# Norm stages merged into the projections behind them, gate tiles in halves, 512-column products and constant products in TensorE's waits

## The chip, the cores and the metric

The kernel runs on one core of one Trainium2 chip. The metric is the device time of one execution in microseconds (us). Three runs of the kernel before gave 1825.0, 1827.96 and 1829.33 us, median 1827.96 us.

## The reference

Two transformer blocks act on x (256 tokens, width 1024), all in float32. What matters here are the places where a norm stands ahead of a projection:

```python
h = x
h = h + hybrid_mixer(rmsnorm(h, norm_mix[l]), w_in[l], ...)      # norm 1 -> projection in_t
h = h + peer_ffn(rmsnorm(h, norm_ffn[l]), peer_wq[l], ...)       # norm 2 -> projection wq
x = rmsnorm(h, norm_final)                                       # final norm
h = jnp.concatenate([meta, x], axis=1)                           # 16 + 256 tokens
u = rms_norm(h, attn_norm_w) @ attn_w_in                         # norm 3 -> projection attn_t
# banded attention with sinks over 16 heads, output (o * silu(gate)) @ w_out, gate = last 1024 columns of u
h = h + attention
u = rms_norm(h, dn_norm_w) @ dn_w_in                             # norm 4 -> projection dn_in
# gated delta rule in chunks of 64 tokens, last product @ dn_w_out
return h[:, 16:]
```

`rmsnorm(x, g)` is `x * rsqrt(mean(x*x) + 1e-6) * g`, by row.

## The kernel before

Every weight matrix is cut into tiles of 128 x 1024 (512 KB) that one ring of four buffers takes in the order of use. ScalarE makes the high part of a tile (`make_high`, L166, a copy to fp32r recorded at L175), VectorE or, for half of the tiles of `dn_in`, GpSimd the low part (`make_low`, L178, L187). Both parts have two buffers. A float32 product is the sum of three fp32r products: high x high, high x low, low x high. `tile_T` (L215) issues them for one weight tile as 16 matmuls on the high part (L222) and 8 on the low part (L226), each with 256 or 272 columns of activations, high or low part. `k.pair(cols)` names the activations' two parts.

The program is a sequence of blocks. A block holds one instruction list for each engine, in the order that the code writes, and no engine goes on to the next block before all are done with this one.

`norm_stage` (L249) is a block of its own, used four times: ScalarE squares each row tile (L271, 128 x 1024 with a running sum), VectorE takes the mean (L288), ScalarE the root (L275, with a load of its table), VectorE refines the inverse root and writes it times the identity (L294 to L300), TensorE multiplies each 128-column chunk of the rows with this diagonal, which turns and scales them (L314, plain fp32; row tile by row tile, chunks inside), and ScalarE and VectorE write the high (L281) and low (L306) parts of the 8 chunks. `early(k, following)` makes the parts of the next projection's first two tiles in the same block, except for the first norm. `project_T` (L320) is the block behind: one `tile_T` for each output chunk, and a copy from PSUM.

`final_norm_stage` (L1368) is another block between `experts_out_stage` (L1255) and norm 3: it loads three arrays, squares the rows (L1386), takes root and Newton step (L1389, `newton` at L1403) and multiplies the rows by root and weight (L1399).

`sink_attention_stage` (L1470) works through 16 units (2 row tiles tt of 128 tokens, 8 pairs of heads each). In iteration u TensorE issues `scores(u + 2)` (L1509), for u < 8 one whole tile of the gate's projection through `tile_T` into bank 7, then `values(u - 1)` (L1536) and `turn(u)` (L1521). ScalarE takes the exponentials (L1605, L1608), makes tile parts, copies the gate tile from PSUM (L1637), stores values and turned scores, and at u = 10 applies Silu to the whole gate (L1644). Units with tt = 1 have more keys, so their matmuls have more columns.

`out_rows` (L2776) is the output projection (L2845, 512 columns), with a residual add by VectorE in two halves of 512 columns (L2829). It runs ahead of norm 2 and of norm 4, and last with the output. `delta_stage` (L1999) ends with the last chunk: `last_within` (L2189), a norm, `last_turn_out` (L2197).

## Time and profile before

| | |
|---|---|
| median of three runs | 1827.96 us |
| the profiled execution | 1824.91 us, span of its trace 1823.0 us |
| granted TensorE clock, mean | 0.949 of full |
| TensorE matmul, weight load | 1672.1 us (92%), 1493.9 us (82%) |
| VectorE, ScalarE, GpSimd | 1183.5 us (65%), 895.0 us (49%), 70.0 us (4%) |
| DMA | 230 MB, mean 126 GB/s |

All times inside the program are counted from the start of the span. The projected and expert tiles follow one another on TensorE almost without a gap; the gaps lie around the norms, in the attention of the second block and at the end of the delta rule. Busy shares are means over the whole program and say little of one stage, so the stages are read by windows and by the order of instructions in time.

### The profile page before, as it was taken

What the parts mean: (1) busy time and instruction counts of PE and PEld (TensorE: products, weight loads), DVE (VectorE), ACT (ScalarE), POOL (GpSimd) and SP (SyncE); (2) the same over time, 40 slices, a digit from 0 to 9 for tenths busy, and PEclk for the clock granted to TensorE, in tenths of its full rate; (3) what the DMA queues carried; (4) which work ended last, traced back from release to release, by engine and by line L of the source; (5) the groups of instructions that cost most, each with busy time, mean ns of one, the idle gap of its engine ahead of it and who ended that gap; (6) DMA issues with size and microseconds to landing.
All of it is one profiled execution on the core that took longest, in us unless ns stands there. A gap on an engine that the chain in (4) does not pass through costs nothing. (4 is left out here: it accounts for less than half of the span.)

```text
span 1823.0 us, 34509 instructions
## 1 busy us (share of the span) xinstructions
PE 1672.1 (92%) x13270; PEld 1493.9 (82%) x13270; DVE 1183.5 (65%) x2021; ACT 895.0 (49%) x1554; POOL 70.0 (4%) x35
## 2 busy tenths in 40 slices
PE   5989988899999999989999999687987999898979
PEld 5978777899999999988888888584656988788877
DVE  3556654478989699976666666544633757546665
ACT  3335543244555677756666666432643644333323
POOL 0000000010000000000000000000000333200000
PEclk9979988999999999999999999796978999999989
DMA  5532143455555444436666656431112444300004
GB/s 181 177 117 82 58 129 124 141 166 169 176 170 173 150 128 128 128 116 194 189 194 194 195 189 193 132 128 35 59 47 69 139 150 151 104 3 3 3 25 138
DMA packets 63078, 230.03 MB, mean 126 GB/s; under 512 B 7009, under 2 KB 7265, under 8 KB 62833
## 3 DMA queue, kind: packets, MB, share of 16 engines
q1 hardware_dynamic: 62960, 228.39, 39.5%
q8 instruction: 83, 1.36, 0.3%
q14 instruction: 35, 0.28, 0.0%
HBM read 227.32 MB, written 1.05 MB: 125 GB/s over the span
## 5 line engine op out<-in xcount | busy, mean ns | idle before, releaser
L974 DVE TENSOR_TENSOR tile_low<-weights,tile_high 128x1024 fp32r<-128x1024 f32 x252 | 307.2, 1222 | 146.4 <-ACT tile_high L964 142.2
L964 ACT ACTIVATE tile_high<-weights 128x1024 fp32r<-128x1024 f32 x252 | 269.1, 1068 | 136.7 <-issue 136.7
L175 ACT ACTIVATE tile_high<-weights 128x1024 fp32r<-128x1024 f32 x169 | 178.1, 1059 | 271.8 <-PE banks L222 106.3
L187 DVE TENSOR_TENSOR tile_low<-weights,tile_high 128x1024 fp32r<-128x1024 f32 x146 | 179.7, 1237 | 187.3 <-ACT tile_high L175 154.2
L222 PE MATMUL banks<-parts,tile_high 128*128 128x272 f32 (+1 forms) x1904 | 266.9, 294 | 14.5 <-PEq L262 6.8
L1026 PE MATMUL banks<-parts,tile_high 128*128 128x256 f32 x2048 | 272.7, 286 | 6.9 <-PEq L900 6.9
L222 PEld LDWEIGHTS banks<-parts,tile_high 128*128 128x128 f32 x1904 | 248.0, 194 | 32.0 <-issue 25.1
L1026 PEld LDWEIGHTS banks<-parts,tile_high 128*128 128x128 f32 x2048 | 257.1, 194 | 7.1 <-issue 7.1
L1308 PE MATMUL banks<-tile_high,parts 128*128 128x512 f32 x1024 | 254.7, 391 | 4.7 <-ACT parts L1288 4.7
L1308 PEld LDWEIGHTS banks<-tile_high,parts 128*128 128x128 f32 x1024 | 193.3, 189 | 45.1 <-issue 4.9
L1031 PE MATMUL banks<-parts,tile_low 128*128 128x256 f32 x1024 | 146.7, 286 | 9.2 <-DVE tile_low L974 9.2
L1031 PEld LDWEIGHTS banks<-parts,tile_low 128*128 128x128 f32 x1024 | 133.0, 193 | 12.3 <-DVE tile_low L974 11.8
L226 PE MATMUL banks<-parts,tile_low 128*128 128x272 f32 (+1 forms) x952 | 137.9, 288 | 0.9 <-DVE tile_low L187 0.9
L1308 PE MATMUL banks<-tile_low,parts 128*128 128x512 f32 x512 | 137.5, 391 | 0.0
L226 PEld LDWEIGHTS banks<-parts,tile_low 128*128 128x128 f32 x952 | 126.8, 192 | 1.1 <-DVE tile_low L187 1.1
L1308 PEld LDWEIGHTS banks<-tile_low,parts 128*128 128x128 f32 x512 | 96.7, 189 | 20.2
L1080 ACT ACTIVATE big<-banks 128x256 f32 (+1 forms) x79 | 52.8, 668 | 120.1 <-PE banks L1031 120.1
L1101 ACT ACTIVATE rows<-rows,kept 128x128 f32<-128x128 f32 x256 | 80.2, 393 | 24.8 <-DVE rows L1182 24.6
L1288 ACT ACTIVATE parts<-big 128x256 fp32r (+1 forms) x128 | 87.6, 686 | 4.3 <-PEq L1007 4.3
L2845 PE MATMUL banks<-tile_high,parts 128*128 128x512 f32 (+1 forms) x288 | 77.4, 417 | 7.2 <-ACT parts L2805 4.1
L1325 DVE TENSOR_TENSOR parts<-big,parts 128x256 fp32r<-128x256 f32 x128 | 81.3, 636 | 1.0 <-ACT parts L1288 1.0
L1182 DVE TENSOR_TENSOR rows<-const,kept 128x1024 f32<-128x1024 f32 x64 | 76.5, 1219 | 0.0
(357 smaller groups left out, 1984.3 us busy)
## 6 DMA issues: line engine op xcount, KB each, us to landing
weights<-in_peer_u SPq DMA_DIRECT2D x128, 512.0 KB, 3.5
weights<-in_peer_v SPq DMA_DIRECT2D x128, 512.0 KB, 3.5
weights<-in_dn_in SPq DMA_DIRECT2D x49, 512.0 KB, 3.5
weights<-in_in_t SPq DMA_DIRECT2D x19, 512.0 KB, 3.6
weights<-in_attn_t SPq DMA_DIRECT2D x19, 512.0 KB, 3.6
weights<-in_in_m SPq DMA_DIRECT2D x16, 512.0 KB, 3.6
weights<-in_wq SPq DMA_DIRECT2D x16, 512.0 KB, 3.5
weights<-in_dn_out SPq DMA_DIRECT2D x16, 512.0 KB, 3.5
```

The lines of the kernel that those rows point to most:

```text
L175: k.nc.scalar.activation(k.high[:, m % 2, :], k.ring.view(n), ACT.Copy).then_inc(*k.high_made.up())
L187: unit.tensor_tensor(k.low[:, m % 2, :], k.ring.view(n), k.high[:, m % 2, :].bitcast(F32), ALU.subtract).then_inc(*k.low_made[engine].up())
L222: ins = nc.tensor.matmul(out, high[:, c, :], rhs(c)[part], start=part + c == 0, stop=False)
L226: ins = nc.tensor.matmul(out, low[:, c, :], rhs(c)[0], start=False, stop=c == chunks - 1)
L964: k.nc.scalar.activation(k.high[:, (s + j) % 2, :], k.ring.buf[:, j % RING, :], ACT.Copy).then_inc(k.high_made.sem, 1)
L974: k.nc.vector.tensor_tensor(k.low[:, (s + j) % 2, :], k.ring.buf[:, j % RING, :], k.high[:, (s + j) % 2, :].bitcast(F32), ALU.subtract).th ...
L1026: ins = nc.tensor.matmul(ps[:, bank, 0:S], high[:, c, :], x[:, c, :], start=part + c == 0, stop=False)
L1031: ins = nc.tensor.matmul(ps[:, bank, 0:S], low[:, c, :], k.pair(S)[0][:, c, :], start=False, stop=c == KC - 1)
L1101: nc.scalar.activation(hot, hot, ACT.Copy, scale=k.chosenT[:, 2, Q * g + q:Q * g + q + 1]).then_inc(*scaled.up())
L1288: nc.scalar.activation(stage[:, j % STAGES, :], c_of(i, j), ACT.Copy).then_inc(staged.sem, 1)
L1308: ins = nc.tensor.matmul(ps[:, 2 * tt + half, :], c[:, j % STAGES, tt * P:tt * P + P], v[:, half, :], start=head and j + part == 0, stop=t ...
L1325: nc.vector.tensor_tensor(stage_low[:, j % STAGES, :], c_of(i, j), stage[:, j % STAGES, :].bitcast(F32), ALU.subtract).then_inc(staged_low ...
```

## The change

- `norm_stage` becomes `norm_programs`, which returns instruction lists; `project_T` and `delta_in_stage` run them at the head of their own block. There is no block boundary between norm and projection, and the first projection tile waits for the parts chunk by chunk.
- The diagonal products run chunk by chunk, row tiles inside (a 16-row tile ahead of them, where there is one). Root and Newton step are taken once for all row tiles, by `newton`.
- `out_rows` squares the halves of the rows right behind the residual adds, makes the first tile of the next projection and loads the table of the root with a one-column Sqrt. `experts_out_stage` does the same, and the whole of what is left of the final norm: it multiplies by the final weight only, squares before and behind it, and the two inverse roots are worked out together in norm 3. The rows are stored without the final norm's factor; the residual add behind the attention multiplies it in.
- `tile_both` replaces `tile_T` where the projection has 256 columns (`in_t`, 19 tiles, `wq`, 16 tiles): both parts of the activations are one moving operand of 512 columns. A sum of the two halves (`tensor_reduce`) replaces the copy from PSUM.
- The gate's tiles in the attention are issued in halves of 12 matmuls (`tile_piece`), one in each of the 16 iterations; Silu runs in iteration 16.
- `keep_busy` issues fp32 matmuls of 384 columns of constants: 3 at the head of norms 2 to 4, 4 behind each of the two `out_rows` ahead of a norm, 8 behind the experts, 5 and 2 in the last chunk.

```diff
+def tile_both(pe, k, n, out, cols, norm=None):
+    x, _ = k.pair(cols)
+    both = k.parts[:, :, 0:KC * cols].rearrange("p a (c n) -> p a c n", c=KC)
+    await_high(pe, k, n)
+    for c in range(KC):
+        if norm is not None:
+            pe.wait_ge(*norm["left"].at(c + 1))
+        ins = nc.tensor.matmul(out[:, 0:2 * cols], high[:, c, :], both[:, :, c, :], start=c == 0, stop=False,
+                               skip_group_check=True)
+    ins.then_inc(*k.high_used.up())
+    await_low(pe, k, n)
+    for c in range(KC):
+        ins = nc.tensor.matmul(out[:, 0:cols], low[:, c, :], x[:, c, :], start=False, stop=c == KC - 1,
+                               skip_group_check=True)
+    tile_used(ins, k, n)
+def sum_halves(k, out, both):
+    return k.nc.vector.tensor_reduce(out, both.rearrange("p (a n) -> p n a", a=2), AX.X, ALU.add)
+def keep_busy(k, bank, times):
+    for _ in range(times):
+        k.nc.tensor.matmul(k.ps[:, bank, 0:3 * P], k.ident, k.common[:, 0:3 * P], start=True, stop=True)
...
+    def scalar(act):
+        if not halves:
...
+        act.wait_ge(*chain.at(3 if scaled_rows else 2 if halves else 1))
+        nc.scalar.activation(root, y, ACT.Sqrt).then_inc(*rooted.up())
+        for m in ahead:
+            make_high(act, k, m)
+        for c in range(KC):
+            act.wait_ge(*turned.at(c + 1))
+            nc.scalar.activation(high[:, c, :], ps[:, c, 0:cols], ACT.Copy,
+                                 scale=weight[:, c:c + 1]).then_inc(*parted.up())
...
+    def tensor(pe):
+        if halves:
+            keep_busy(k, 7, 3)
+        if t > NT:
+            pe.wait_ge(*scaled.at(1))
             for c in range(KC):
+                product(0, c)
+        pe.wait_ge(*scaled.at(t))
+        for c in range(KC):
+            for i in range(t - NT, t):
+                ins = product(i, c)
+            ins.then_inc(*turned.up())
...
@@ experts_out_stage, ScalarE and VectorE behind the last round
+            act.wait_ge(*got.at(32))
+            nc.scalar.activation(scratch[0:META, 0, :], k.hm[0:META, :], ACT.Square,
+                                 accum_out=sums[0:META, 0:1]).then_inc(*squared.up())
+            nc.scalar.activation(k.norms[:, 47:48], k.ident[:, 0:1], ACT.Sqrt).then_inc(*squared.up())
+            make_high(act, k, k.tiles["attn_t"])
+            for tt in range(NT):
+                act.wait_ge(*added.at(tt + 1))
+                nc.scalar.activation(scratch[:, tt, :], k.h[:, tt, :], ACT.Square,
+                                     accum_out=sums[:, 1 + NT + tt:2 + NT + tt]).then_inc(*squared.up())
+            for tt in range(NT):
+                act.wait_ge(*weighted.at(tt + 1))
+                nc.scalar.activation(scratch[:, tt, :], k.h[:, tt, :], ACT.Square,
+                                     accum_out=sums[:, 1 + tt:2 + tt]).then_inc(*squared.up())
...
+            for tt in range(NT):
+                dve.wait_ge(*squared.at(3 + tt))
+                nc.vector.tensor_tensor(k.h[:, tt, :], k.h[:, tt, :], wide, ALU.mult).then_inc(*weighted.up())
+            make_low(dve, k, k.tiles["attn_t"])
...
@@ sink_attention_stage
-                if u < fills:
-                    if u:
-                        pe.wait_ge(*gated.at(u))
-                    tile_T(pe, k, gate_tile(u), fill, lambda c: (high[:, c, :], low[:, c, :]))
+                if u < 2 * fills:
+                    if u and u % 2 == 0:
+                        pe.wait_ge(*gated.at(u // 2))
+                    tile_piece(pe, k, gate_tile(u // 2), fill, lambda c: (high[:, c, :], low[:, c, :]), u % 2, 2)
...
-                if u == fills + 2:
+                if u == len(units):
                     act.wait_ge(*gated.at(fills))
                     nc.scalar.activation(T[:, GATE:GATE + fills, :], T[:, GATE:GATE + fills, :],
                                          ACT.Silu).then_inc(*gated.up())
...
@@ delta_stage, TensorE, last chunk
             for b in range(2):
                 last_within(b)
+            keep_busy(k, 0, 5)
             for b in range(2):
                 last_turn_out(b)
+            keep_busy(k, 0, 2)
...
@@ out_rows (send is None ahead of norms 2 and 4)
+            if send is None:
+                make_high(act, k, k.tiles[following])
+                nc.scalar.activation(k.norms[:, 47:48], k.ident[:, 0:1], ACT.Sqrt).then_inc(*squared.up())
+                for half in range(2):
+                    for i, (h, _, rows, _) in enumerate(tiles):
+                        act.wait_ge(*added.at(len(tiles) * half + i + 1))
+                        nc.scalar.activation(scratch[0:rows, half, i, :], h[0:rows, 512 * half:512 * half + 512], ACT.Square,
+                                             accum_out=k.norms[0:rows, 40 * half + i:40 * half + i + 1]).then_inc(*squared.up())
...
+                if half == 0 and send is None:
+                    make_low(dve, k, k.tiles[following])
...
+            if send is None:
+                keep_busy(k, 7, 4)
```

On TensorE, from the end of the first block's output projection to the first tiles of `wq`, the order was, before (L2845 output projection, L314 diagonal products of norm 2, L222 and L226 the tiles of `wq`):

```order
L2845 MATMUL banks<-tile_high,parts 128x512 x8
L2845 MATMUL banks<-tile_low,parts 128x512 x4
L2785 UNCONDITIONAL_BRANCH
L309 UNCONDITIONAL_BRANCH
L314 MATMUL banks<-rows 128x128 x16
L262 UNCONDITIONAL_BRANCH
L335 UNCONDITIONAL_BRANCH
L222 MATMUL banks<-parts,tile_high 128x256 x16
L226 MATMUL banks<-parts,tile_low 128x256 x8
```

and is now (L2932 output projection, L281 `keep_busy`, L368 diagonal products, L245 and L250 `tile_both`):

```order
L2932 MATMUL banks<-tile_high,parts 128x512 x8
L2932 MATMUL banks<-tile_low,parts 128x512 x4
L281 MATMUL banks<-const 128x384 x4
L2857 UNCONDITIONAL_BRANCH
L402 UNCONDITIONAL_BRANCH
L281 MATMUL banks<-const 128x384 x3
L368 MATMUL banks<-rows 128x128 x16
L245 MATMUL banks<-parts,tile_high 128x512 x8
L250 MATMUL banks<-parts,tile_low 128x256 x8
```

One block boundary (two branches) is gone, seven constant matmuls have come, and a tile has 16 matmuls instead of 24.

On ScalarE at the same place, before (L175 tile parts, L2805 activations' parts, L271 squares, L275 root, L281 parts of the normed rows):

```order
L2805 ACTIVATE parts<-big 128x512
L175 ACTIVATE tile_high<-weights 128x1024 x2
L2785 UNCONDITIONAL_BRANCH
L268 UNCONDITIONAL_BRANCH
L271 ACTIVATE rows,small<-rows 128x1024 x2
L275 ACT_TABLE_LOAD
L275 ACTIVATE small<-small 128x1 x2
L175 ACTIVATE tile_high<-weights 128x1024 x2
L281 ACTIVATE parts<-banks,param 128x256 x8
```

and now (L2882 one-column Sqrt, L2887 squares of halves, L331 root, L336 parts):

```order
L2877 ACTIVATE parts<-big 128x512
L175 ACTIVATE tile_high<-weights 128x1024 x3
L2882 ACT_TABLE_LOAD
L2882 ACTIVATE norms<-const 128x1
L2887 ACTIVATE rows,norms<-rows 128x512 x4
L2857 UNCONDITIONAL_BRANCH
L424 UNCONDITIONAL_BRANCH
L331 ACTIVATE norms<-norms 128x2
L175 ACTIVATE tile_high<-weights 128x1024
L336 ACTIVATE parts<-banks,param 128x256 x8
```

Table load, squares and one tile's parts stand ahead of the boundary now; behind it are one root, one tile's parts and the eight chunks.

On TensorE in the attention, iterations 9 and 10 (tt = 1) were, before (L1536 values, L1521 turned scores, L1509 scores):

```order
L1509 MATMUL banks<-big 128x272 x2
L1536 MATMUL banks<-big 64x128 x6
L1521 MATMUL banks<-const,big 16x128 x2
L1521 MATMUL banks<-const,big 128x128 x4
L1509 MATMUL banks<-big 128x272 x2
L1536 MATMUL banks<-big 64x128 x6
```

and are now (L1574 scores, L270 the gate's tile in halves, L1599 values, L1586 turned scores):

```order
L1574 MATMUL banks<-big 128x272 x2
L270 MATMUL banks<-parts,tile_high 128x272 x4
L270 MATMUL banks<-parts,tile_low 128x272 x8
L1599 MATMUL banks<-big 64x128 x6
L1586 MATMUL banks<-const,big 16x128 x2
L1586 MATMUL banks<-const,big 128x128 x4
L1574 MATMUL banks<-big 128x272 x2
L270 MATMUL banks<-parts,tile_high 128x272 x12
L1599 MATMUL banks<-big 64x128 x6
```

Twelve matmuls of a gate tile stand between scores and values in the second half of the units, where none stood; in the first half twelve stand where 24 stood.

## Rows read from the trace of the kernel before

**Rows 1.** Waits of TensorE: who for whom, us in total, times, longest.
```profile
PE banks L314 <- DVE rows L300: 44.9, 4, 15.7
...
PE banks L2197 <- DVE rows L2440: 4.4, 1, 4.4
```
**Rows 2.** Windows: length, busy (count) of PE, PEld, DVE, ACT, POOL, clock, DMA, GB/s.
```profile
812.00:1164.00 352.00, 350.75 (x1536) 289.95 (x1536) 225.83 (x255) 209.65 (x254) 0.00 (x0) 0.99 0.61 191
1310.00:1350.00 40.00, 31.62 (x172) 19.18 (x172) 19.68 (x72) 22.54 (x64) 0.00 (x0) 0.83 0.00 1
```
**Rows 3.** Timeline around norm 2: start, length, engine, instructions, [idle before and releaser].
```profile
286.98 1.28 DVE L2829 TENSOR_TENSOR rows<-rows,banks 128x512 f32<-128x512 f32 x2 [1.43 <-PE banks L2845]
...
290.77 1.28 ACT L275 ACT_TABLE_LOAD   x1
...
293.42 6.45 PE L314 MATMUL banks<-rows 128*128 128x128 f32 x32 [6.47 <-DVE rows L300]
...
301.82 3.33 PE L222 MATMUL banks<-parts,tile_high 128*128 128x256 f32 x16 [1.96 <-PEq L262]
...
306.26 2.08 PE L222 MATMUL banks<-parts,tile_high 128*128 128x256 f32 x16
...
309.14 2.08 PE L222 MATMUL banks<-parts,tile_high 128*128 128x256 f32 x16
```
**Rows 4.** Timeline, fp32 matmuls of 272 columns ahead of the attention, two records each.
```profile
1241.52 9.33 PE L1453 MATMUL banks<-big,const 20*64 20x272 f32 x40 [4.58 <-DVE big L1413]
```
**Rows 5.** Timeline around norm 1.
```profile
14.76 5.87 PE L314 MATMUL banks<-rows 128*128 128x128 f32 x32 [14.76 <-DVE rows L300]
...
15.25 0.35 DVE L300 TENSOR_SCALAR rows<-const,small 128x128 f32<-128x128 f32 x1
...
27.12 2.08 PE L222 MATMUL banks<-parts,tile_high 128*128 128x256 f32 x16
```
**Rows 6.** Timeline from the experts over final norm and norm 3.
```profile
1163.57 2.35 DVE L1334 TENSOR_TENSOR rows<-rows,banks 128x1024 f32<-128x1024 f32 x2 [3.88 <-PE banks L1308]
...
1166.22 1.06 ACT L1386 ACTIVATE rows<-rows 128x1024 f32<-128x1024 f32 x1 [7.88 <-PEq L1270]
...
1169.72 0.20 ACT L1389 ACTIVATE small<-small 128x2 f32<-128x2 f32 x1
...
1170.75 0.16 DVE L1413 TENSOR_TENSOR small<-small 128x2 f32<-128x2 f32 x1
...
1194.06 2.16 PE L222 MATMUL banks<-parts,tile_high 128*128 128x272 f32 x16
```
**Rows 7.** Timeline of TensorE in the attention: a gate tile, then units without one.
```profile
1275.53 2.27 PE L222 MATMUL banks<-parts,tile_high 128*128 128x272 f32 x16
...
1278.73 1.51 PE L1536 MATMUL banks<-big 16*64 16x128 f32 x8
...
1313.98 1.95 PE L1536 MATMUL banks<-big 16*64 16x128 f32 x12 [0.43 <-ACT big L1619]
...
1317.78 1.95 PE L1536 MATMUL banks<-big 16*64 16x128 f32 x12 [0.43 <-ACT big L1619]
...
1324.69 3.39 PE L1536 MATMUL banks<-big 16*64 16x128 f32 x12 [3.55 <-ACT big L1619]
...
1330.60 3.39 PE L1536 MATMUL banks<-big 16*64 16x128 f32 x12
```
**Rows 8.** The same timeline of ScalarE: Silu of the gate.
```profile
1319.04 2.02 ACT L1644 ACTIVATE big<-big 128x2176 f32<-128x2176 f32 x1
```
**Rows 9.** Timeline around norm 4.
```profile
1387.99 1.87 DVE L2829 TENSOR_TENSOR rows<-rows,banks 16x512 f32<-16x512 f32 x3 [2.30 <-PE banks L2845]
...
1412.58 2.16 PE L222 MATMUL banks<-parts,tile_high 128*128 128x272 f32 x16
```
**Rows 10.** Timeline of TensorE in the last projection.
```profile
1772.85 3.75 PE L2845 MATMUL banks<-tile_high,parts 128*128 128x512 f32 x8 [1.87 <-ACT parts L2805]
...
1777.57 2.01 PE L2845 MATMUL banks<-tile_high,parts 128*128 128x512 f32 x8
```

More of the change, by code:

```diff
@@ L258, in norm_stage @@
     starts = [sum(rows for _, rows in tiles[:i]) for i in range(len(tiles))]
[L259 to L260 removed]
+    t = len(tiles)
+    n = t + NT if scaled_rows else t
+    sums, y, root, inv, step = (k.norms[:, 8 * a:8 * a + n] for a in range(5))
+    scratch = k.mid[:, (3 - t) * D:3 * D].rearrange("p (t n) -> p t n", n=D)
     diagonal = lambda i: scratch[0:tiles[i][1], i, 0:tiles[i][1]]
[L262 to L269 removed]
+    ahead = range(k.tiles[following] + (1 if halves else 0), k.tiles[following] + AHEAD)
```

269 lines of the change are left out of this document (137 added, 132 removed).

## The prediction

> **What bounds the kernel now.** The busy shares come first: TensorE is busy 92% of the span, every other engine far less, so time is won where TensorE stands idle, runs at the lower clock, or issues more than it must. The list of its waits comes next. Its largest entry by far is norm: the diagonal products waited 44.9 us in all for VectorE's diagonals, four times [rows 1]. The windows then tell good stretches from bad ones. In the second half of the experts TensorE is busy 350.75 of 352 us at clock 0.99 [rows 2]: 1536 matmuls of 512 columns, 0.229 us each, and 191 GB/s of weights come in behind them. In the second half of the attention it is busy 31.62 of 40 us, at 0.83 [rows 2]. The timeline around one norm shows what a wait is made of: the output projection ends where VectorE begins its last adds, 286.98, and the second tile of `wq` starts at 306.26 [rows 3]. Between lie adds, squares, a table load of 1.28 us, root and Newton step, products at 0.40 us each (6.45 us for 16), the last parts, a block boundary, and a first tile that takes 4.4 us where its successor takes 2.88 (306.26 to 309.14) [rows 3]. The products and that first tile ran at the lower of the clock's two levels, 1.2 GHz, after TensorE had idled.
>
> **Unit prices.** A projection tile of 24 matmuls with 256 columns takes 2.88 us [rows 3], 0.120 each; one with 512 columns costs 0.229 [rows 2]. An fp32 matmul is two records; 40 records of 272 columns take 9.33 us [rows 4], 0.86 ns a column and record, so a product of 128 columns costs 0.22 us at the upper clock, and one of `keep_busy` with 384 columns 0.66. A block boundary costs 0.3 us (VectorE ends at 1165.92, ScalarE starts at 1166.22) [rows 6]. From the root's start to the end of the Newton step are 1.2 us (1169.72 to 1170.91) [rows 6]; a small VectorE step in a chain 0.2; a diagonal 0.35 [rows 5], a second one chained behind it 0.6 for both.
>
> **Norm 2.** The last add ends at 288.26 [rows 3]. ScalarE squares the last half behind it, 0.7 us (half of L1386's 1.06 and the read of the sum [rows 6]), to 289.0. The four constant matmuls run from 286.95 to 289.6 and so set the end of the block; they cost 0.6 us. With the boundary it is 289.9. Two small steps, root and Newton, two diagonals: 0.45 + 1.2 + 0.6, products from 292.15. They are 16 x 0.22 = 3.5 us at the upper clock, since three constant matmuls fill 289.9 to 291.9. Parts are made beside them, chunk by chunk, and the first tile's parts are there. Its first matmul comes at 295.7, its end 8 x 0.229 + 8 x 0.120 = 2.8 us later at 298.5, against 306.26. **7.7 us.** If the upper clock does not hold, the products take their old 6.45 us and the tile up to 1.5 more: 3.3 us are left.
>
> **Norm 1.** Nothing changes ahead of it, and it has no constant matmuls. Products wait for both diagonals, 0.5 us later than 14.76, and take 5.87 as before [rows 5], to 21.1. The wait for the last parts, a boundary, and the late making of the first tile's parts go: tile 0 ends at 23.9, against 27.0 [rows 5]. **3.1 us.** Its weights are among the first four tiles, which the input block already loads.
>
> **512 columns.** A tile goes from 2.88 to 2.79 us by these prices. The mean over 1536 matmuls holds the stage's start and loop turns, so I take 0.227 and 2.77: 0.11 x 33 further tiles = 3.6, less 0.5 for two sums at projection ends that are longer than copies. **3.1 us.** VectorE has a low part of 1.2 us and a sum of about 0.7 in each tile and stays hidden. Weights must come at 189 GB/s, below the 191 of the experts [rows 2].
> The Trainium skill, page "TensorE: Matmul & The Clock Gate", section "Back-to-back issue gap", gives N/2.4 + 2.5 ns for a matmul. By it 8 matmuls of 512 columns in place of 16 of 256 would save only 8 x 2.5 ns = 0.02 us a tile, under 1 us in all. Rows 2 and 3 disagree: both widths carry 13 to 16 ns over their columns at 2.4 GHz. By the rule the sum would be 3 us smaller.
>
> **Final norm and norm 3.** TensorE stops at 1163.5; adds end at 1165.92 [rows 6]. The square of the first row tile (1.1) runs beside the second add, that of the second ends at 1167.1. VectorE weights both tiles (1.2 each, as its adds) to 1168.4, ScalarE squares the second by 1169.6; VectorE's low part ends there too. Eight constant matmuls end at 1168.8 and are covered. Boundary: 1169.9. Three small steps, root, Newton, three diagonals 0.65 + 1.2 + 0.9: 1172.7. The eight products of the 16-row tile start at 1172.2 and take 1.8 us, the 16 others 3.5: 1177.5. The first tile, 24 x 0.125 = 3.0, ends at 1180.5, against 1194.06 [rows 6]. **13.5 us.** It goes to 10.5 if the products run at the lower clock. The loads move: final weight and meta rows are fetched 350 us earlier, ahead of the experts' fifth tile, when four tiles lie ready; the block of constants goes ahead of `attn_t`'s fifth tile.
>
> **Attention.** A unit with tt = 1 has 3.37 us of matmuls (period 3.80 from 1313.98 to 1317.78, less the wait of 0.43) [rows 7]. Silu (2.02 us [rows 8] and two table loads) holds the exponentials back: TensorE waits 3.55 us, and comes back at the lower clock, two units at 5.91 us (1324.69 to 1330.60) instead of 3.37 [rows 7]. Window 1310 to 1350 thus holds 8.4 us idle and 2 x 2.54 = 5.1 of slow clock [rows 2, 7]. Half gate tiles fill the waits: what stood in the first half, where TensorE was full, now stands here. Of 13.5 us I take off 2: cutting tiles in two costs something (a gate tile takes 3.20, 1275.53 to 1278.73 [rows 7], 0.2 more than the 3.0 of 24 x 0.125 elsewhere, paid at most once more for each of eight tiles), and nothing stands behind the last unit to fill its wait. Silu now runs behind the last copy, 1.28 + 2.02 + the last store 0.3, where values took 2.3: the block ends 1.3 us later. **10 us.** VectorE has peaks and scale, 2.5 to 3.0 us a unit, and every second unit 1.2 more; a unit lasts 4.1 to 5.0, so TensorE stays the bound. If the chain over make_high and make_low does bind in the first half, 1 us in each of 8 units comes back: down to 2.
>
> **Norm 4.** As norm 2 with three row tiles: last add 1389.86 [rows 9], square and boundary to 1391.0, chain 0.45 + 1.2 + 0.9, eight small products (1.8, half of them beside the diagonals) and 16 others (3.5) to 1398.3, first tile to 1401.3, against 1412.46 [rows 9]. **11.2 us**; 7 at the lower clock.
>
> **Last chunk.** Five constant matmuls, 3.3 us, stand in the wait of 4.4 us for the norm [rows 1], and two, 1.3 us, ahead of the wait of 1.87 for the next parts [rows 10]. The first tile of the last projection takes 4.7 us (1772.85 to 1777.57) [rows 10], a warm one 2.72. **2 us**, or nothing.
>
> **Sum:** 7.7 + 3.1 + 3.1 + 13.5 + 10 + 11.2 + 2 = 50.6 us. The profiled execution took 1824.9 us, 3 below the median of 1828.0; taken off the median it gives 1777.4, off this execution 1774.3. I forecast **1777 us**.
>
> **Rivals.**
> *A: the clock falls all the same.* TensorE then works through norms 2 to 4 and the last tile at 1.2 GHz: 4.4 + 3 + 4.2 + 2 = 13.6 us less gained, 1791. (4.4 is 7.7 less 3.3.) For it: in norm 2 the clock fell again behind products that had just ended, within 2 us of idleness [rows 3]. Against it: the constants leave gaps of 0.3 and 1.3 us only, and fp32 products brought the clock back in norm 1. Chance 0.17. The skill's page, section "Part 1: The HAM clock gate", says that activity releases the throttle and that its phase is not tied to the kernel; the traces agree with the first, and the second would put A between runs rather than in all.
> *B: attention's chain binds.* ScalarE's high part waits behind exponentials, VectorE's low part behind it, peaks behind that; TensorE waits about 1 us a unit: 8 us less, 1785. Against it: the same chain stood in every iteration before, with a whole tile to make in each, and the list of waits has no entry of that size for it. Chance 0.13.
> *C: 512 columns save nothing* by a per-matmul cost of 3 ns instead of 13: 1780. Chance 0.10.
> *D: slower.* The moving operand is two pieces of 256 columns that lie apart; no row here shows such an operand. Were it streamed at half rate, each of 280 matmuls would cost 0.227 us more, 64 us in all: 1841. It decides from 0.18 us more a matmul. The sum over two strided halves would add to that. Chance 0.02.
> *E: the table of the root is lost* between the one-column Sqrt and the root, so 3 loads of 1.28 return: 1781. Against it: the order lists no load there. Chance 0.03.
> The forecast as it stands has 0.55.
>
> **Numbers.** The forecast's own bounds are 1770 (boundaries and waits also gone elsewhere, cheaper attention) to 1784. The range of 1766 to 1791 takes in B, C, E and A's middle. A measurement tells about 0.2%, 3.7 us, from no change; all cases but D lie far below: faster 0.97, same 0.01, slower 0.02.
>
> **What would show it.** Right: TensorE's first tile starts 5.5 to 6 us behind the boundary of norms 2 and 4, 7.5 behind that of norm 3, with granted clock near 1; tile periods of 2.77 us in `in_t` and `wq`; attention from first gate matmul to last values about 75 us instead of 86; no wait for exponentials over 1 us. Wrong: diagonal products at 0.43 us each (A), waits of the turned scores on VectorE in every unit (B), periods of 2.88 (C) or above 4 us (D), a table load ahead of the root (E).

## The result, and the profile after

The changed kernel took 1779.01 us (median of four runs, 1776.18 to 1780.42) against 1826.74 us for the kernel before, measured in turn with it (1825.0 to 1829.33): a ratio of 0.9736, 95% interval 0.9718 to 0.9754. The forecast was 1777 us: 50.6 us taken off the first median of the kernel before, 1827.96; the two medians here differ by 47.7. The profiled execution took 1776.18 us, with a span of 1774.4 us (before: 1823.0) and a mean granted clock of 0.971 (before: 0.949).

The list of TensorE's waits, as in [rows 1]. The four waits for diagonals, 44.9 us, have become two, of which one is the start of the program:

```profile
PE banks L368 <- DVE rows L356: 17.2, 2, 15.3
...
PE banks L2200 <- DVE big L2402: 7.1, 5, 2.0
```

The other of the two is the 1.89 us at norm 4. Around norm 2, to set beside [rows 3], the timeline of TensorE and VectorE reads:

```profile
281.57 2.74 PE L281 MATMUL banks<-const 128*128 128x384 f32 x8
281.77 1.28 DVE L2914 TENSOR_TENSOR rows<-rows,banks 128x512 f32<-128x512 f32 x2 [0.30 <-PE banks L2932]
...
284.61 2.17 PE L281 MATMUL banks<-const 128*128 128x384 f32 x6 [0.30 <-PEq L2857]
...
286.84 3.84 PE L368 MATMUL banks<-rows 128*128 128x128 f32 x32
...
290.44 2.09 PE L245 MATMUL banks<-parts,tile_high 128*128 128x512 f32 x8
...
293.32 2.00 PE L245 MATMUL banks<-parts,tile_high 128*128 128x512 f32 x8
...
296.11 2.00 PE L245 MATMUL banks<-parts,tile_high 128*128 128x512 f32 x8
```

The products take 3.84 us for 32 records (6.45 before), the first tile starts 5.83 us behind the boundary at 284.61, and tiles follow at 2.79 us (293.32 to 296.11). Norm 3, to set beside [rows 6], has the same picture: constants, 48 records of products in 5.72 us, and the second tile at 1165.15. In norms 2 to 4 no table load stands between the one-column Sqrt and the root.

```profile
1147.73 5.32 PE L281 MATMUL banks<-const 128*128 128x384 f32 x16
...
1154.31 2.17 PE L281 MATMUL banks<-const 128*128 128x384 f32 x6 [1.26 <-PEq L1347]
...
1156.53 5.72 PE L368 MATMUL banks<-rows 16*128 16x16 f32 x48
```

Norm 4 does not. Here VectorE, GpSimd and TensorE in order of time, to set beside [rows 9]:

```profile
1351.38 3.58 POOL L1898 MEMSET big<- 128x768 f32 x4 [769.83 <-POOLq L2857]
...
1351.62 0.54 DVE L352 TENSOR_SCALAR norms<-norms 128x3 f32<-128x3 f32 x1
...
1352.49 0.18 DVE L1470 RECIPROCAL norms<-norms 128x3 f32<-128x3 f32 x1 [0.34 <-ACT norms L331]
1352.70 0.16 DVE L1472 TENSOR_TENSOR norms<-norms 128x3 f32<-128x3 f32 x1
...
1353.10 1.88 DVE L1476 TENSOR_SCALAR norms<-norms 128x3 f32<-128x3 f32 x1
...
1355.49 7.35 PE L368 MATMUL banks<-rows 16*128 16x16 f32 x48 [1.89 <-DVE rows L356]
...
1365.73 2.17 PE L227 MATMUL banks<-parts,tile_high 128*128 128x272 f32 x16
```

A step of three numbers a partition takes 1.88 us where its neighbours take 0.16 to 0.18. It ends at 1354.98, where the fourth fill by GpSimd ends (1351.38 + 3.58 = 1354.96). The step of 0.54 us ends at 1352.16 with the first fill, which takes 0.76 us. TensorE runs out of constants, idles 1.89 us, and its products take 7.35 us instead of norm 3's 5.72: the granted clock is 1.00 up to 1357 and 0.50 from 1359 to 1361. In the kernel before, the same fills ran behind the norm, beside the first tile of `dn_in` (1407.97):

```profile
1407.93 0.62 POOL L1830 MEMSET rows<- 48x640 f32 x1 [812.19 <-POOLq L262]
1408.51 3.55 POOL L1833 MEMSET big<- 128x768 f32 x4
```

In the attention, to set beside [rows 2, 7], the window of the second half, and three of TensorE's rows near its end:

```profile
1270.00:1310.00 40.00, 37.94 (x261) 27.48 (x259) 23.39 (x73) 25.99 (x69) 0.00 (x0) 1.00 0.11 36
```
```profile
1303.29 1.95 PE L1599 MATMUL banks<-big 16*64 16x128 f32 x12
...
1307.08 1.95 PE L1599 MATMUL banks<-big 16*64 16x128 f32 x12 [1.09 <-ACT big L1682]
1312.39 4.86 PE L2932 MATMUL banks<-tile_high,parts 128*16 128x512 f32 x11 [3.36 <-ACT parts L2877]
```

TensorE is busy 37.94 of 40 us at clock 1.00 (before: 31.62 at 0.83), and the one wait for an exponential or turned score that is left, ahead of the last values, takes 1.09 us.

Read off at the same events in both traces, the stretches changed by these amounts (us):

| stretch | before | after | gained | predicted |
|---|---|---|---|---|
| start to second tile of `in_t` (norm 1) | 27.12 | 24.24 | 2.9 | 3.1 |
| the further tiles of `in_t` and `wq` (512 columns) | 53.95 + 44.14 | 52.66 + 43.11 | 2.3 | 3.1 |
| last output matmul to second tile of `wq` (norm 2) | 19.70 | 11.99 | 7.7 | 7.7 |
| last experts' matmul to second tile of `attn_t` (final norm, norm 3) | 30.92 | 17.66 | 13.3 | 13.5 |
| first scores to output projection (attention) | 90.49 | 79.83 | 10.7 | 10 |
| last output matmul to second tile of `dn_in` (norm 4) | 25.02 | 17.79 | 7.2 | 11.2 |
| last projection to the end | 50.17 | 48.32 | 1.9 | 2 |

They add up to 46.0 us; the spans differ by 48.6. The other 2.6 us are the first experts' block, which the change leaves alone and which took 448.1 us before and 445.5 after; it is taken up below. (Of the stretches between, the mixer's is 1.1 us shorter and the one between `wq` and the experts 0.9 longer; these nearly cancel.)

### The profile page after: what moved, and what is told of

The parts are those of the page before. It is cut to its first block and busy times, and to the rows that moved or that the text cites. A ratio compares the mean times of both kernels' runs of the same rounds, so it can differ in the third digit from the quotient of the medians.

```text
span 1774.4 us, 34027 instructions
## 1 busy us (share of the span) xinstructions
PE 1666.5 (94%) x13054; PEld 1470.4 (83%) x13054; DVE 1192.9 (67%) x2003; ACT 894.6 (50%) x1559; POOL 70.0 (4%) x35
## 5 line engine op out<-in xcount | busy, mean ns | idle before, releaser
L175 ACT ACTIVATE tile_high<-weights 128x1024 fp32r<-128x1024 f32 x169 | 178.0, 1057 | 258.2 <-issue 78.7
L1100 PEld LDWEIGHTS banks<-parts,tile_high 128*128 128x128 f32 x2048 | 255.6, 193 | 8.0 <-issue 8.0
L227 PE MATMUL banks<-parts,tile_high 128*128 128x272 f32 (+1 forms) x1216 | 170.3, 293 | 4.2 <-PEq L442 3.4
L227 PEld LDWEIGHTS banks<-parts,tile_high 128*128 128x128 f32 x1216 | 157.0, 191 | 19.3 <-issue 16.8
L1105 PEld LDWEIGHTS banks<-parts,tile_low 128*128 128x128 f32 x1024 | 131.7, 192 | 12.3 <-DVE tile_low L1048 11.8
L231 PE MATMUL banks<-parts,tile_low 128*128 128x272 f32 (+1 forms) x608 | 88.0, 287 | 0.9 <-DVE tile_low L187 0.9
L2932 PE MATMUL banks<-tile_high,parts 128*128 128x512 f32 (+1 forms) x288 | 75.6, 410 | 7.6 <-ACT parts L2877 4.4
L231 PEld LDWEIGHTS banks<-parts,tile_low 128*128 128x128 f32 x608 | 80.6, 189 | 1.1 <-DVE tile_low L187 1.1
```

Source lines behind the costliest of these rows:

```text
L175: k.nc.scalar.activation(k.high[:, m % 2, :], k.ring.view(n), ACT.Copy).then_inc(*k.high_made.up())
L227: ins = nc.tensor.matmul(out, high[:, c, :], rhs(c)[part], start=part + c == 0, stop=False)
L231: ins = nc.tensor.matmul(out, low[:, c, :], rhs(c)[0], start=False, stop=c == chunks - 1)
L1100: ins = nc.tensor.matmul(ps[:, bank, 0:S], high[:, c, :], x[:, c, :], start=part + c == 0, stop=False)
L1105: ins = nc.tensor.matmul(ps[:, bank, 0:S], low[:, c, :], k.pair(S)[0][:, c, :], start=False, stop=c == KC - 1)
L2932: ins = nc.tensor.matmul(ps[0:rows, bank + half, :], xs[:, place(q), c0:c0 + rows][:, c, :], w[:, c, :], start=q + part + c == 0, stop=q = ...
```

## The experiments

Every kernel below is compared with the kernel before, run in turn with it on the same chip. Since chips and executions differ by a few us, each comparison between two variants rests first on the stretches of their profiles. Those around the norms and in the attention repeat to 0.1 us where nothing differs; the first experts' block and the chunk loop of the delta rule do not, as shown below. A stretch is read from one profiled execution of each kernel.

**The change again.** No edit.

> The changed kernel again, as the base of the others on this chip: 1779 us within 3, a ratio of 0.972 to 0.975 to the kernel before. In norm 4 the third step of the Newton chain, a TENSOR_SCALAR on 128x3, takes 1.9 us again (0.17 in norm 3), TensorE waits about 1.9 us for the diagonals, and its clock falls within the diagonal products. If that long step was an accident of the one profiled execution, it is back at 0.17 us here.

1780.09 us, ratio 0.9765 (0.9749 to 0.9781), a little above the 0.972 to 0.975 expected: the kernel before took 1822.05 us here, so the gain was 42.0 us in place of 47.7. The long step of norm 4 is back, so it was no accident. All stretches of the table repeat to 0.15 us: 11.99 for norm 2, 17.64 for norm 3, 79.84 for the attention, 17.79 for norm 4. What differs lies elsewhere: the first experts' block took 448.0 us. The windows of its first 12 us, of the changed kernel's first profile and then of this one:

```profile
351.67:363.67 12.00, 12.00 (x88) 12.00 (x89) 7.24 (x27) 5.78 (x7) 6.89 (x1) 0.86 0.46 145
```
```profile
352.36:364.36 12.00, 12.00 (x79) 12.00 (x80) 6.34 (x23) 4.91 (x7) 6.89 (x1) 0.76 0.39 131
```

The same code behind the same kind of wait (7.85 and 7.38 us) got the upper clock back sooner in one execution than in the other, which is worth about 1 us. The rest of the difference lies behind a wait of 2.90 us in the middle of the block: the granted clock over the 4 us around the restart was 1.00 in the first execution (599.3 to 603.3) and 0.57 in the second (600.0 to 604.0), 1.5 us of time. So the 2.6 us that the sum lacked are no effect of the change: the same kernel shows them against itself.

**GpSimd's fills behind the norm.**

```diff
-            for ap in (k.vT[:, :, 0, :, 0:PAD], k.kT[:, :, 0, :, 0:PAD], k.dq[:, :, 0, 0:PAD], k.state):
-                nc.gpsimd.memset(ap, 0.0).then_inc(*cleared.up())
             pool.wait_ge(*norm["turned"].at(KC))
             nc.gpsimd.memset(dup[0:48], 0.0).then_inc(*clear.up())
+            for ap in (k.vT[:, :, 0, :, 0:PAD], k.kT[:, :, 0, :, 0:PAD], k.dq[:, :, 0, 0:PAD], k.state):
+                nc.gpsimd.memset(ap, 0.0).then_inc(*cleared.up())
```

> GpSimd's four fills with zeros are issued behind the diagonal products of norm 4 instead of at the head of the block. Theory 1 (the fills hold up VectorE's TENSOR_SCALARs in norm 4): the two long steps fall from 0.54 and 1.88 us to 0.17, the diagonals are ready 2.1 us earlier, TensorE's wait goes, the clock stays up in the products (16 at 0.22 us in place of 7.35 us for all), the second tile of dn_in starts 3.5 to 4 us earlier against the last add, and the run is about 4 us faster than the changed kernel, near 1775. Rival (the long steps come from something else, such as the read of instructions or ScalarE's work beside them): they stay long and the time does not move.

1775.56 us, ratio 0.9741 (0.9721 to 0.9761), 4.5 us below the change on the same chip; the two intervals overlap, and the stretch decides. Norm 4 takes 14.19 us in place of 17.79, 3.6 less. Its rows:

```profile
1356.14 0.17 DVE L1476 TENSOR_SCALAR norms<-norms 128x3 f32<-128x3 f32 x1
...
1356.94 5.72 PE L368 MATMUL banks<-rows 16*128 16x16 f32 x48
...
1363.30 3.56 POOL L1900 MEMSET big<- 128x768 f32 x4
```

The step is back at 0.17 us, TensorE's wait is gone, and the products take the 5.72 us of norm 3. With 14.19 the term would have been 10.8 of the 11.2 predicted.

**Other forms of the same steps.** The fills stay where the change has them; in norm 4 alone VectorE's steps with one operand in SBUF are written with two.

```diff
-            done(nc.vector.tensor_scalar(y, sums, 1.0 / D, EPS, ALU.mult, ALU.add))
+            done(nc.vector.scalar_tensor_tensor(y, sums, 1.0 / D, k.norms[:, 45:46].broadcast_to([P, n]), ALU.mult, ALU.add))
...
+            done(nc.vector.scalar_tensor_tensor(step, step, -0.5, k.norms[:, 44:45].broadcast_to([P, n]), ALU.mult, ALU.add))
...
+                nc.vector.scalar_tensor_tensor(diagonal(i), k.ident[0:rows, 0:rows], inv[0:rows, i:i + 1],
+                                               k.ident[0:rows, 0:rows], ALU.mult, ALU.mult).then_inc(*scaled.up())
```

> The change with GpSimd's four fills where the change has them, but in norm 4 the VectorE steps with one SBUF operand (mean, Newton's two scalings, the diagonals) written with two SBUF operands: the same values, and two constants come from two columns set in norm 3. Theory: a VectorE instruction with one tensor operand cannot run beside a fill by GpSimd and one with two can. Then no VectorE step between the root and the products takes over 0.3 us (1.88 us in the change), the products do not wait for the fills to end, and the distance from the end of the output projection to norm 4's second tile is about 14.2 us, as with the fills put later, in place of 17.8; the fills may take a little longer. Rival: the fills themselves (memory of the same partitions, or the order of the block) slow VectorE whatever its form; then the distance stays at 17 to 18 us. Time 1776 or 1779.5.

Its rows, while the fills run:

```profile
1354.97 3.55 POOL L1915 MEMSET big<- 128x768 f32 x4 [773.35 <-POOLq L2874]
...
1356.32 0.16 DVE L361 SCALAR_TENSOR_TENSOR norms<-norms 128x3 f32<-128x3 f32 x1
...
1357.12 5.72 PE L385 MATMUL banks<-rows 16*128 16x16 f32 x48
```

Norm 4 takes 14.19 us, as with the fills moved. The fills as such do not slow VectorE: reciprocal, `TENSOR_TENSOR` and `SCALAR_TENSOR_TENSOR` ran beside them at 0.16 to 0.18 us in both kernels, and only `TENSOR_SCALAR` waited for a fill to end. The theory as it was written was too wide: reciprocal has one tensor operand too, and did not wait. The Trainium skill, page "SBUF — State Buffer", section "Who interferes with whom", has the rule: VectorE and GpSimd share one pair of ports as an exclusive lock; `tensor_scalar` may take it, and two operands in SBUF contend with a GpSimd that reads SBUF, not with one that only writes. The traces agree in each of its cases that occur here, down to an operand of three elements a partition.

The whole kernel, though, took 1780.86 us, ratio 0.9761 (0.9742 to 0.9781), which is the change's own time: 1776 had been expected. The stretch from norm 4's second tile to the last projection took 365.0 us, in place of the 360.4 of the change and of the kernel with the fills moved. TensorE at its fourth `solve` in the chunk loop, in this kernel and then in the one with the fills moved:

```profile
1675.24 2.81 PE L2217 MATMUL banks<-big 64*64 64x128 f32 x32 [2.00 <-DVE big L2419]
1677.98 3.68 PE L2222 MATMUL banks<-big 64*128 64x64 f32 x32
```
```profile
1673.58 1.98 PE L2200 MATMUL banks<-big 64*64 64x128 f32 x32 [2.01 <-DVE big L2402]
```

The instructions and the wait of 2.0 us are the same; here the clock fell behind it (windows of 3 us show a granted clock of 0.50 to 0.54 from 1676 to 1685), there it did not. The intervals from one `solve` to the next give the whole account. Of the five waits ahead of `solve`, the clock fell in this kernel behind the third (1.5 us of time) and the fourth (4.7 us). In the change and in the kernel with the fills moved it fell behind the fifth alone (1.6 us). 6.2 less 1.6 are the 4.6 us.

The new forms are not the cause. The kernel with Silu last (below) has the change's own forms and an unchanged chunk loop, and its stretch took 365.0 us as well, with falls behind the same two waits. The window of its fourth `solve`:

```profile
1677.37:1707.37 30.00, 26.89 (x494) 24.54 (x494) 16.82 (x42) 7.05 (x11) 0.00 (x0) 0.83 0.01 2
```

The kernel with whole tiles, whose loop is unchanged too, took 357.7 us. The experiment with constants in the chunk loop takes this up.

**Without constant matmuls.** `keep_busy` issues none.

> All matmuls of constants left out (they are no part of the result). Theory 1 (the constants keep TensorE's clock up): products of norms 2 to 4 at 0.43 us each again, 3 to 3.5 us lost in norm 2, 3 to 4 in norm 3, 0 to 2 in norm 4 (there the clock falls as it is), 2 in the last chunk with its first tile back at 4.7 us: 8 to 13 us slower than the changed kernel, 1787 to 1792. Rival (merging alone keeps the gaps short enough): within 3 us of the changed kernel.

1786.04 us, ratio 0.98 (0.9778 to 0.9822), 6.0 us above the change and short of the 8 to 13 expected. By stretches the constants are worth 1.1 us in norm 2, 3.4 in norm 3, 1.4 in norm 4 and 1.7 at the end, 7.6 in all. TensorE at norm 2:

```profile
287.79 5.47 PE L368 MATMUL banks<-rows 128*128 128x128 f32 x32 [4.63 <-DVE rows L356]
```

The products take 5.47 us, not the 6.45 of [rows 3], and behind them the clock is up: the first tile (2.07 us for its high part) is no slower than with constants. So rival A's price of 13.6 us for the clock, taken from the waits of before, was nearly twice what it costs once the waits are as short as the merge makes them.

**256 columns again.** `in_t` and `wq` through `tile_T`, with copies in place of the sums.

```diff
-                if n == S:
+                if False:
                     tile_both(
```

> The projections in_t and wq use matmuls of 256 columns and a copy again; all else of the change stays. Theory 1 (fixed cost of 13 ns a matmul): tile period 2.88 us instead of 2.79, 35 tiles, 3 us slower, less 0.5 for the shorter copies: 2 to 3 us slower than the changed kernel. Rival by the fixed cost of 2.5 ns that the Trainium skill's page TensorE: Matmul & The Clock Gate states: under 1 us.

1778.63 us, ratio 0.9763 (0.9745 to 0.9781): the whole time cannot tell it from the change. The stretches can: 53.95 and 44.14 us, exactly those of before, against 52.66 and 43.11. Two neighbouring tiles of `wq` follow at 2.88 us (297.12 to 300.00):

```profile
297.12 2.08 PE L227 MATMUL banks<-parts,tile_high 128*128 128x256 f32 x16
...
300.00 2.08 PE L227 MATMUL banks<-parts,tile_high 128*128 128x256 f32 x16
```

Eight matmuls fewer save 0.09 us a tile, 11 ns each. Each matmul has a weight load of its own, so the 11 ns belong to the two together; no run takes them apart. The 512 columns are worth 2.3 us, and 0.13 more in the first tile of `wq` (norm 2 takes 12.12 us here).

**The attention as before.** Whole gate tiles in the first eight iterations and Silu at the tenth; and the same with Silu in the last iteration.

```diff
-                if u < 2 * fills:
-                    if u and u % 2 == 0:
-                        pe.wait_ge(*gated.at(u // 2))
-                    tile_piece(pe, k, gate_tile(u // 2), fill, lambda c: (high[:, c, :], low[:, c, :]), u % 2, 2)
+                if u < fills:
+                    if u:
+                        pe.wait_ge(*gated.at(u))
+                    tile_T(pe, k, gate_tile(u), fill, lambda c: (high[:, c, :], low[:, c, :]))
...
-                if u == len(units):
+                if u == fills + 2:
```

The last two lines of the edit are the first kernel's alone. Both kernels also go back to the earlier order of tile parts, banks of values and waits for them; what these are worth counts with the halves.

> The change with the attention's iterations as they were before: whole gate tiles in the first 8 iterations, Silu in iteration 10, late rather than last. Theory: the halves fill waits, so the stretch from the first gate tile to the first tile of the output projection goes back from 79.8 us to about 90.5, TensorE waits some 3.5 us for an exponential behind Silu and runs two units at the lower clock there, and the time rises by about 10.7 us over the change, to 1790. Rival: the gain in this stretch came from something else (the clock at its start, the merged norms), then the stretch stays below 85 us and the time below 1785.

> As the kernel with whole tiles, but Silu in the last iteration, as in the change. It splits the attention's gain in two. Theory: most of it is the Silu stall: 3.55 us of idleness and two units of 5.91 us in place of 3.37 go (8.6 us), less 1.3 us for Silu at the end, so the stretch takes about 83.5 us and the time is about 1783 to 1784; the filling of the waits by halves is worth the other 3 to 4 us. Rival: the halves do it (without gate matmuls in the second half TensorE waits 0.4 us or more in every unit and its clock falls there), then the stretch stays near 90 us.

The first took 1791.62 us, ratio 0.9826 (0.9798 to 0.9855), and the stretch 90.21 us: halves and Silu's place together are worth 10.4 us, as thought. The second took 1788.36 us, ratio 0.9791 (0.9763 to 0.9818), and the stretch 86.39. Silu's move is worth 3.8 us, not 8.6 less 1.3, and the halves 6.6, not 3 to 4. (Of the whole time, expected at 1783 to 1784, less can be said: in the profiles the second kernel's chunk loop took 365.0 us against 357.7 in the first, which hides the 3.8.) TensorE's rows, of the first kernel and then of the second:

```profile
1299.36 3.39 PE L1601 MATMUL banks<-big 16*64 16x128 f32 x12 [3.54 <-ACT big L1684]
...
1305.27 3.39 PE L1601 MATMUL banks<-big 16*64 16x128 f32 x12
...
1311.18 2.05 PE L1601 MATMUL banks<-big 16*64 16x128 f32 x12
```
```profile
1306.62 0.82 PE L1586 MATMUL banks<-const,big 128*16 128x128 f32 x6
1308.54 3.03 PE L1601 MATMUL banks<-big 16*64 16x128 f32 x12 [1.09 <-ACT big L1684]
...
1313.86 1.95 PE L1601 MATMUL banks<-big 16*64 16x128 f32 x12 [1.09 <-ACT big L1684]
...
1318.19 3.39 PE L1601 MATMUL banks<-big 16*64 16x128 f32 x12 [1.09 <-ACT big L1684]
```

Without the stall the clock still falls, now behind two of the three waits of 1.09 us in the last units, which have no scores to issue any more (in the first kernel the same waits left it up: 1.95 us for the values behind each). The half gate tiles fill the first two of these, and the 0.43 us in each unit ahead of them; the last one stays in the change. My split of the term was wrong both ways, and its sum right.

**More constants.** The fills moved, six constant matmuls at the head of norm 1, three behind the attention, three in place of four behind the two output projections.

```diff
-        if halves:
-            keep_busy(k, 7, 3)
+        keep_busy(k, 7, 3 if halves else 6)
...
+            keep_busy(k, 0, 3)
...
-                keep_busy(k, 7, 4)
+                keep_busy(k, 7, 3)
```

> The change with GpSimd's fills behind the first matmuls of the block (3.6 us, as measured before), 6 constant matmuls ahead of the products of norm 1, 3 behind the attention's last values and 3 in place of 4 behind the two output projections. Theory: norm 1's products come at the upper clock, 3.7 us in place of 6.2, and the output projection's first tile behind the attention takes 2.8 us in place of 5.3; one constant matmul less makes the stretch ahead of norms 2 and 4 up to 0.6 us shorter. Together 5 us less than with the fills alone: 1770 to 1772, the fastest version. Rival: the constants only take the place of the waits and the clock does not come up in time at the very start of the program (other matmuls there are few); then norm 1 stays at 6.2 us and the time is 1773 to 1775.

1769.49 us, ratio 0.9694 (0.9675 to 0.9713). Start of the program, then the output projection behind the attention:

```profile
8.77 6.77 PE L281 MATMUL banks<-const 128*128 128x384 f32 x12 [8.77 <-PEq L493]
15.38 3.82 PE L368 MATMUL banks<-rows 128*128 128x128 f32 x32
```
```profile
1309.50 2.20 PE L281 MATMUL banks<-const 128*128 128x384 f32 x6
1313.56 2.95 PE L2932 MATMUL banks<-tile_high,parts 128*16 128x512 f32 x12 [1.86 <-ACT parts L2877]
```

The expectation was 1770 to 1772. Norm 1's second tile starts at 22.06 in place of 24.24. That its products had run at the lower clock is read from their pace, 6.27 us for 32 records against 3.82 here; the granted clock reads 1.00 at the start of the program in both profiles, even over these constants, which take 0.56 us a record against 0.34 at norm 2. The output projection takes 33.23 us in place of 35.55, while the stretch ahead of it is 0.6 longer: 1.7 net. One constant less is worth 0.5 us at norm 2, nothing at norm 4.

**Constants in the chunk loop.** On the kernel with the other forms, whose clock had fallen there, three constant matmuls ahead of each of the five `solve`; then on the kernel with more constants, with three more in the scores block, in the wait ahead of the experts.

```diff
             def solve(c):
+                keep_busy(k, 0, 3)
...
                 tile_used(ins, k, first + q)
+            pe.wait_ge(*taken.at(2))
+            keep_busy(k, 0, 3)
```

The first line added is in both, the others in the second kernel alone.

> The kernel with other forms in norm 4, and 3 constant matmuls (2.0 us) ahead of each of the five products of the inverse (`solve`) in the chunk loop of the delta rule, where TensorE waits 2.0 us for VectorE. That kernel won 3.6 us in norm 4 and yet took as long as the change, and in its profile the granted clock fell behind two of these waits, to half for some 9 us at one of them, where the same stretch of the change ran at full clock. Theory: the same pattern of waits lets the clock fall in one execution and not in another; with the waits filled it falls in none, and the stretch from norm 4's second tile to the first tile of the last projection takes 358 to 360.5 us in place of 365.0, the whole about 1776. Rival: the difference of 4.6 us comes from something else that the new forms do (then it stays at 1780 and the stretch at 365), or the constants come late and push the chunk loop on by up to 0.7 us each, up to 3.5 in all.

> The kernel with more constants (1769.5 us), the same 3 constant matmuls ahead of each `solve`, and 3 more at the end of the scores block, in TensorE's wait of 7.2 us for four copies by VectorE ahead of the experts. Theory: the experts' first tile takes 2.1 us for its high part in place of 3.75 and 1.1 for its low part in place of 1.6, 2 us less, and the chunk loop gains up to 1.8 us, what the fall of the clock behind its fourth wait cost in that kernel's profile: 1766 to 1767.5. Rival: the clock comes up too late for the experts' first tile, since two thirds of the wait stay idle, and the chunk loop gains nothing: 1769 to 1770.

The first took 1778.26 us, ratio 0.9736 (0.9722 to 0.975). Windows of the same 30 us, as a distance from norm 4's second tile, in the kernel with other forms and in this one:

```profile
1665.72:1695.72 30.00, 26.89 (x493) 24.56 (x494) 16.83 (x43) 7.07 (x11) 0.00 (x0) 0.83 0.01 2
```
```profile
1663.61:1693.61 30.00, 28.90 (x596) 25.68 (x596) 17.59 (x44) 9.19 (x21) 0.00 (x0) 1.00 0.01 3
```

The clock holds, and the stretch is 362.0 us in place of 365.0, yet not 358 to 360.5. From one `solve` to the next the last three constants cost 0.05 us each, the first two 1.5 to 1.6: there TensorE waits 0.5 us only, not 2.0. The second kernel took 1774.55 us, ratio 0.9709 (0.9692 to 0.9725), against 1769.49 and 0.9694 (0.9675 to 0.9713) without these constants on another chip: no gain, and by the ratios no clear loss. Its stretch over the chunk loop takes 360.8 us in place of 359.2 (3.1 us for the first two, less 1.6 for a fall that did not come behind the last). The experts start 1.4 us later, behind constants that ran at the lower clock, and their block takes 1.9 us less:

```profile
348.14 3.81 PE L281 MATMUL banks<-const 128*128 128x384 f32 x6 [4.49 <-DVE big L1006]
352.24 2.14 PE L1101 MATMUL banks<-parts,tile_high 128*128 128x256 f32 x16 [0.30 <-PEq L973]
```

Both times were missed. The runs gave the place of the loss, and with it the last version.

**Constants ahead of the late `solve` only**, and the kernel with more constants once more beside it.

```diff
             def solve(c):
+                if c > 1:
+                    keep_busy(k, 0, 3)
```

> The kernel with more constants, with 3 constant matmuls ahead of `solve` only from its third call on, where TensorE waits 2.0 us; ahead of the first two it waits 0.5 us, and constants there pushed the chunk loop on by 1.5 us each. Theory: the stretch from norm 4's second tile to the first tile of the last projection takes 357.7 us in place of 359.2 to 360.8 (no fall of the clock behind the last wait, 1.6 us, less 0.15 for three delays of 0.05), and never the 365.0 that falls behind the third and fourth wait made; the time is 1.5 us below that of the kernel with more constants on the same chip, and its runs lie closer together. Rival: the clock falls in spite of the constants, then the stretch is 359 us or more.

> The kernel with more constants once more, as the one to compare with on the same chip: 1769.5 us as before, within 3 us for a chip of its own.

1766.68 us, ratio 0.9675 (0.9662 to 0.9688), the fastest of all versions: 3.3% below the kernel before and, by the ratios, 0.6 to 0.9% below the change's two measurements, on other chips. The stretch took 357.8 us, as expected, against 359.2 in the kernel beside it, which took 1767.49 us (0.9682, 0.9668 to 0.9695). The 1.5 us are plain in the profiles, where the clock fell behind the last wait in the one and not in the other. The medians differ by 0.8, within their intervals, where 1.5 was expected, and the runs do not lie clearly closer together (4.1 us apart against 4.5).

## Why the prediction was right, and where it was not

The time came out 2 us over the forecast and inside its own bounds, no rival took place as it was priced, and of seven terms five were right to 0.7 us. Some of this closeness is luck: the seven terms gave 46.0 of 50.6 us, and in the profiled execution 2.6 us came from the clock in the first experts' block, which the change does not touch. In the repeat the time was again 3 us over the forecast, but the gain over the kernel before only 42.0 us. Each stretch around a norm also holds several edits at once (merge, chunk order, squares and table load ahead); of these only the constants were taken apart, so that the merge as such brought the rest is worked out from the rows and not shown by a run.

- **Norm 2, norm 1, final norm and norm 3** came out as worked: 7.7, 2.9 and 13.3 us for 7.7, 3.1 and 13.5. The first tile started 5.8 us behind norm 2's boundary and 7.7 behind norm 3's (1154.31 to 1162.01), with products at the upper clock.
- **Norm 4** is the term that was mis-sized: 7.2 us for 11.2. The step that failed is "chain 0.45 + 1.2 + 0.9", built "as norm 2 with three row tiles". It held VectorE's and ScalarE's steps alone, and did not ask what else the merged block starts at the same moment. Before, the block of `dn_in`, and with it GpSimd's fills, began behind the norm; the merge put them beside the chain. Moving them gave 3.6 us back, and other forms of the same steps did so too; 0.4 of the 4.0 stays unexplained. That the prediction has "7 at the lower clock" for this term is a coincidence: the first part of the products ran at the upper clock, and about half of the loss was TensorE's wait. Its sign "5.5 to 6 us behind the boundary" did not fit its own sum for norm 4 either, which has 7.3 us from 1391.0 to 1398.3; measured were 11.2, and 7.6 with the fills moved.
- **512 columns** were worth 2.3 us for 3.1. I took 2.77 us a tile where the prices of [rows 2, 3] gave 2.79, and 2.79 it is; 33 times 0.02 is 0.7. Rival C did not hold: 11 ns saved for each matmul removed, with its weight load, stand nearer to the 13 to 16 of the rows than to 2.5. The Trainium skill, page "TensorE: Matmul & The Clock Gate", section "Back-to-back issue gap", gives the 2.5 ns for an isolated matmul.
- **Attention** gained 10.7 us for 10. The waits went as said (79.8 us in all; 74.5 from first scores to last values), and rival B's wait did not come: from 1276 to 1307 TensorE waits for nothing. But which edit brought how much was wrong, as the two experiments show: Silu's place 3.8 us and the halves 6.6.
- **Last chunk** was 1.9 us for 2, nearly all of it by constants (without them 1.7 of it is gone).
- **Rival A** had the clock fall in spite of the constants, for 13.6 us. In norms 2 and 3 it did not. In norm 4 it did for part of the products, behind the idle time that the fills had made. The runs without constants put their whole worth at 6 to 7.6 us.
- **Not priced:** the first tile behind the attention still ran at the lower clock (0.54 from 1312 to 1318), and so, by their pace, did norm 1's products, these as predicted; constants there were worth 1.7 and 2.2 us more.

One thing stays open: why the clock falls behind one wait of 2.0 us and not behind the same wait in another kernel. The experiments show that it does, that it did not ahead of any `solve` whose wait was filled, and what it costs, no more. The Trainium skill, page "TensorE: Matmul & The Clock Gate", section "Part 1: The HAM clock gate", says that the gate's phase is not tied to the kernel; the repeat of the change and these chunks are in keeping with that.

## What to carry to other kernels

When blocks are merged, write down for every engine what now starts at the same moment, the idle ones too: a fill that no one waited for cost 3.6 us because a step of three numbers could not pass it. Put constant work only into waits that are about as long as it, reading each instance of a wait by itself: the same three matmuls (2.2 us) cost 0.05 us in a wait of 2.0 us and 1.5 in one of 0.5. And where totals spread by 3 us or more, judge an edit by the stretch between two fixed events.

## What the runs showed of the hardware that was not expected

- GpSimd's four fills held up a VectorE `TENSOR_SCALAR` of 128 x 3 for 1.7 us, while reciprocal and two-operand forms of the same size ran beside them in 0.16 to 0.18.
- The same program behind the same kind of wait ran at clock 0.76 or 0.86 over the next 12 us, and behind a wait of 2.90 us at 0.57 or 1.00 over 4 us, 2.6 us of time together. In the chunk loop falls behind waits of 2.0 us cost 6.2 us in two kernels and 1.6 in others with the same loop.
- Without constants, fp32 products behind 4.6 us of idle time took 5.47 us for 32 records, neither the 3.84 of the upper clock nor the 6.45 seen before.
